# Turning the input before its root is known, and multiplying every projection by it later

## What is computed

```
h = concatenate([meta, x])                      # (272, 2048)
u = h * rsqrt(mean(h*h, axis=-1) + EPS) * attn_norm_w
z = u @ w_in[l]                                 # (272, 12368)
hq, hf, hi, hg, aq, ak, av, iq, ik, iw, ga, gb = split_cols(z, IN_SIZES)
...                                             # recurrence, indexer, attention
m = sigmoid(ga) * (y_h @ w_branch_hgrn) + sigmoid(gb) * (y_a @ w_branch_dsa)
h = h + m @ w_out
...                                             # conv-gated MLP, final norm
```

## Time and profile before

| | us |
|---|---|
| median of 3 runs (1610.62 to 1610.81) | 1610.77 |
| the profiled execution | 1610.73 |
| its span in the trace | 1609.0 |
| PE busy | 1594.9 |
| DVE busy | 961.0 |
| ACT busy | 711.3 |
| POOL busy | 94.1 |

### The profile page before, as it was taken

How to read it: one execution, slowest core, us unless ns; L and a number is a source line. 1 busy time by engine, 2 the same in 40 slices (tenths; PEclk the granted TensorE clock), 3 DMA queues, 4 the chain that set the end, 5 groups by cost and what they waited for, 6 DMA issues and landing times.

```text
span 1609.0 us, 29434 instructions
## 1 busy us (share of the span) xinstructions
PE 1594.9 (99%) x12214; PEld 1536.5 (95%) x12214; DVE 961.0 (60%) x1117; ACT 711.3 (44%) x750; POOL 94.1 (6%) x152
## 2 busy tenths in 40 slices
PE   8999999999999999999999999999999999999998
PEld 8999999999999999999999999999889999999886
DVE  7555778853355556766656666665445666666453
ACT  6333554544443335654345555454333334334332
POOL 1100050000000001111320000000000000000000
PEclk9999999999999999999999999999999999999999
DMA  7655565555464554476655555554555656465551
GB/s 236 206 158 166 163 197 177 181 174 161 153 202 158 178 165 130 144 256 218 198 179 181 186 177 188 183 182 170 196 194 174 208 161 204 159 206 190 202 208 54
DMA packets 244966, 290.36 MB, mean 180 GB/s; under 512 B 5665, under 2 KB 231186, under 8 KB 244498
## 3 DMA queue, kind: packets, MB, share of 16 engines
q1 hardware_dynamic: 238114, 278.78, 52.9%
q0 software_dynamic: 2176, 6.34, 1.2%
q10 hardware_dynamic: 4608, 4.23, 0.8%
HBM read 283.02 MB, written 6.32 MB: 180 GB/s over the span
## 4 chain that ended last, share of the span: by engine, by line
PE 98%; DVE 1%; ACT 0%; DMA 0%; issue 0%; SPq 0%; DVEq 0%; ACTq 0%
PE ps L618 24%; PE ps L619 24%; PE ps L620 24%; PE ps L1002 5%; PE ps L999 5%; PE ps L1001 5%; PE ps L948 2%; PE ps L946 2%; PE ps L947 2%; PE ps L740 1%; PE ps L715 0%; PE ps L841 0%; PE ps L938 0%; DMA x_tok<-in_x_dram 0%; PE ps L770 0%; PE ps L750 0%
## 5 line engine op out<-in xcount | busy, mean ns | idle before, releaser
L618 PE MATMUL ps<-u_hi,w_hi 128*128 128x258 f32 (+2 forms) x2944 | 841.5, 286 | 0.0
L619 PE MATMUL ps<-u_lo,w_hi 128*128 128x258 f32 (+2 forms) x2944 | 834.2, 283 | 0.0
L620 PE MATMUL ps<-u_hi,w_lo 128*128 128x258 f32 (+2 forms) x2944 | 833.8, 283 | 0.0
L1348 DVE TENSOR_TENSOR w_lo<-raw,w_hi 128x2048 fp32r<-128x2048 f32 x259 | 595.6, 2300 | 363.6 <-ACT w_hi L1043 363.3
L1043 ACT ACTIVATE w_hi<-raw 128x2048 fp32r<-128x2048 f32 x259 | 496.2, 1916 | 573.7 <-PE ps L620 408.4
L618 PEld LDWEIGHTS ps<-u_hi,w_hi 128*128 128x128 f32 x2944 | 556.0, 189 | 4.7 <-DVE z_qf L1448 2.5
L619 PEld LDWEIGHTS ps<-u_lo,w_hi 128*128 128x128 f32 x2944 | 555.9, 189 | 0.3
L620 PEld LDWEIGHTS ps<-u_hi,w_lo 128*128 128x128 f32 x2944 | 555.7, 189 | 0.0
L999 PE MATMUL ps<-w_hi,hid_hi 128*128 128x512 f32 x352 | 137.8, 391 | 0.0
L1002 PE MATMUL ps<-w_lo,hid_hi 128*128 128x512 f32 x352 | 137.1, 390 | 0.0
L1001 PE MATMUL ps<-w_hi,hid_lo 128*128 128x512 f32 x352 | 137.0, 389 | 0.0
(11 more groups left out here) (290 smaller groups left out, 1295.8 us busy)
## 6 DMA issues: line engine op xcount, KB each, us to landing
raw<-in_w_in_dram SPq DMA_DIRECT2D x48, 2048.0 KB, 8.4
raw<-in_w_ffn_gate_dram SPq DMA_DIRECT2D x22, 2048.0 KB, 8.0
raw<-in_w_ffn_up_dram SPq DMA_DIRECT2D x22, 2048.0 KB, 8.0
raw<-in_w_ffn_down_dram SPq DMA_DIRECT2D x20, 2048.0 KB, 7.7
raw<-in_w_out_dram SPq DMA_DIRECT2D x8, 2048.0 KB, 8.8
raw<-in_w_branch_hgrn_dram SPq DMA_DIRECT2D x8, 1024.0 KB, 5.4
raw<-in_w_branch_dsa_dram SPq DMA_DIRECT2D x8, 1024.0 KB, 8.5
gate_spill<-gate_st ACTq DMA_DIRECT2D x32, 129.0 KB, 3.6
```

The lines of the kernel that those rows point to most:

```text
L618: mm(acc, w_hi[s][:, k, :], mov_hi(k), start=(k == first), stop=False)
L619: mm(acc, w_hi[s][:, k, :], mov_lo(k), start=False, stop=False)
L620: ins = mm(acc, w_lo[s][:, k, :], mov_hi(k), start=False, stop=(k == last))
L1348: v.tensor_tensor(w_lo[m % 4][:], raw[(m // 2) % 2][:, :, P * (m % 2):P * (m % 2) + P], w_hi[m % 4][:].bitcast(F32), ALU.subtract).then_in ...
```

## The change

The sum of a projection is multiplied by the root where it is taken out of PSUM, so the blocks are turned and split without it.

* **Opening.** L1366, L1380, L1371, L1374 and POOL's L486 go. Meta tokens are turned first, 16 transposes into four banks, weighted by DVE into `u_meta` (4 instructions of 64 columns) and split in one step each by ACT and DVE. A "part" n of `x_part` is what ACT rounds and DVE takes the rest of at once: parts 1 to 7 are the first tile's blocks 0 to 6 (128 wide), 8 to 14 the second tile's, 15 to 23 the blocks 7 to 15 with both tiles (256 wide). The banks are seven, and the key sum moves to the eighth. Warming matmuls shrink from 18 + 4 to 2 + 4 + 2.
* **Panels in halves.** The key panel and the first query panel are each two DMAs of 8 blocks. ACT rounds the key panel in two instructions; DVE takes the first rest, POOL the second. The low-weight products of the key's second half stand behind all of its high ones, and so do those of unit 2's first half.
* **The root.** ACT squares `x_tok1` after rounding unit 3, DVE squares `x_tok2` between the halves of unit 2; one root instruction for the three tiles; DVE builds three diagonals (`diag`), PE spreads them over the partitions in one product with ones (`spread_roots`, inside unit 3), DVE copies that to `x_rs` (128 x 272).
* **Taking out.** L1394, L1414, L1448, L1482, L1483, L1617 and L1637 become products with `x_rs` instead of copies. The gates are scaled by POOL (`scale_gates`, 16 instructions of 128 x 516) when they are back from HBM.
* **Moved.** The vectors' transposes (L682) go from the front of unit 2 into unit 3, `key_squares` from unit 3 into unit 4; DVE's `rest(4)` stands ahead of the vector work instead of behind it. SP issues panel 2 when POOL and DVE have taken the key rests. `gate_st` lies elsewhere, and ACT waits for `forget_ready` before the gate units.

The diff, cut to its core:

```diff
+        def x_bank(k):
+            return ps[(k % EARLY + 4) % 7]
+        def x_part(n):
+            if n <= EARLY:
+                return n - 1, x_bank(n - 1)[:, 0:P], slice(META, END)
+            if n <= 2 * EARLY:
+                return n - EARLY - 1, x_bank(n - EARLY - 1)[:, 2 * P:3 * P], slice(END, T)
+            return n - EARLY - 1, x_bank(n - EARLY - 1)[:, 0:2 * P], slice(META, T)
...
+            sp.wait_ge(key_lo, 1)
             load(2, 0, w_cols[:, :, C_IQ + 256:C_IQ + 512])
...
-            pool.wait_ge(x_rstd, 3)
-            pool.tensor_scalar(x_tok[2][:, D // 2:], x_tok[2][:, D // 2:], rstat[:, 2:3], None, ALU.mult)\
-                .then_inc(half_normed, 1)
+            pool.wait_ge(hi_ready, 2)
+            pool.tensor_tensor(w_lo[0][:, 8:KT, 0:KEYS], raw[0][:, 8:KT, 0:KEYS], w_hi[0][:, 8:KT, 0:KEYS].bitcast(F32),
+                               ALU.subtract).then_inc(lo_ready, 2)
...
+            def scale_gates(slot, count):
+                pool.wait_ge(gate_in[slot], count)
+                pool.tensor_tensor(gates[slot][:], gates[slot][:],
+                                   x_rs[:, T0:T].rearrange("p (a t) -> p a t", a=1).to_broadcast([P, 2, TQ]), ALU.mult)\
+                    .then_inc(gate_scaled, 1)
...
+            for k in range(8):
+                keys_high(k)
+                if k + 11 < KT:
+                    turn_rest(k + 11)
+                if k == 1:
+                    pe.wait_ge(key_lo, 1)
+                    keys_low(0)
+                if k >= 1:
+                    keys_low(k)
+            pe.wait_ge(hi_ready, 2)
+            for k in range(8, KT):
+                keys_high(k)
+            pe.wait_ge(lo_ready, 2)
+            for k in range(8, KT):
+                ins = keys_low(k)
+            ins.then_inc(projected, 2)
...
+            project(3, 3, 1, T0, ((0, 3), (3, 10), (10, KT)), (spread_roots, turn_vectors))
+            pe.wait_ge(z_free, 5)
+            project(4, 0, 0, T0, ((0, 8), (8, KT)), (key_squares,))
...
+            for n in range(EARLY + 1, KT + EARLY + 1):
+                if n == 2 * EARLY:
+                    act.wait_ge(key_in, 16)
+                    round_keys(slice(0, 8))
+                if n == 2 * EARLY + 2:
+                    act.wait_ge(landed[0], landed_by[0])
+                    round_keys(slice(8, KT))
+                if n == KT + EARLY:
+                    act.wait_ge(query_in, 16)
+                    activation(w_hi[2][:, 0:8, :], raw[1][:, 0:8, 0:P], ACT.Copy).then_inc(hi_half, 1)
+                round_x(n)
...
-                v.tensor_copy(iq[:, n - U_IQ, :], ps[n % 2][:, 0:TQ]).then_inc(z_free, 1)
+                v.tensor_tensor(iq[:, n - U_IQ, :], ps[n % 2][:, 0:TQ], x_rs[:, T0:T], ALU.mult).then_inc(z_free, 1)
```

More of the change, by code:

```diff
@@ L162, in hybrid_block @@
         iq_st = [at(f"iq_st{a}", STG + 1024 * a, [P, SEQ]) for a in range(2)]
-        gate_st = [at(f"gate_st{a}", R[7] + 6144 + 1032 * a, [P, TQ]) for a in range(2)]
+        gate_st = [at(f"gate_st{a}", R[3] + 6144 + 1032 * a, [P, TQ]) for a in range(2)]
         qkv_st = at("qkv_st", STG, [P, 3, T])
@@ L639, in warm_up @@
                 for _ in range(n):
-                    mm(ps[0][:, 0:P], ones[:], ones[:], start=True, stop=True)
+                    mm(ps[7][:, 0:P], ones[:], ones[:], start=True, stop=True)
             pe.wait_ge(consts, 4)
@@ L644, in _ @@
             pe.wait_ge(norm_in, 16)
[L645 to L683, removed]
+            nc.tensor.transpose(ps[6][:, 0:KT], vec_rows[0:KT, 0, :], ident[0:KT, 0:KT]).then_inc(norm_turned, 1)
+            warm_up(2)
+            def turn(out, t, k):
+                return nc.tensor.transpose(out, x_tok[t][:, P * k:P * k + P], ident[:])
@@ new lines, in _ @@
+            pe.wait_ge(meta_zeroed, 1)
+            pe.wait_ge(x_in[0], 16)
+            for b in range(4):
+                for k in range(4):
+                    ins = turn(ps[b][:, P * k:P * k + P], 0, 4 * b + k)
+                ins.then_inc(meta_turned, 1)
+            warm_up(4)
+            pe.wait_ge(norm_ready, 1)
+            pe.wait_ge(x_in[1], 16)
+            for k in range(EARLY):
+                if k >= 3:
+                    pe.wait_ge(meta_weighted, k - 2)
+                turn(x_bank(k)[:, 0:P], 1, k).then_inc(x_turned, 1)
@@ new lines, in _, with keys_high, keys_low @@
+            keys_acc = ps[7][0:KEYS, 0:T]
+            def keys_high(k):
+                pe.wait_ge(ul_ready, k + EARLY + 1)
+                mm(keys_acc, w_hi[0][:, k, 0:KEYS], u_hi[:, k, :], start=(k == 0), stop=False)
+                mm(keys_acc, w_hi[0][:, k, 0:KEYS], u_lo[:, k, :], start=False, stop=False)
+            def keys_low(k):
+                return mm(keys_acc, w_lo[0][:, k, 0:KEYS], u_hi[:, k, :], start=False, stop=(k == KT - 1))
+            for k in range(EARLY, EARLY + 4):
+                turn_rest(k)
@@ new lines, in _, with turn_vectors, spread_roots @@
+            ins.then_inc(projected, 2)
+            def turn_vectors():
+                pe.wait_ge(vec_in, 16 * 10)
+                for n, rows in enumerate((V_A, V_B, V_C)):
+                    ins = nc.tensor.transpose(ps[4 + n][:, 0:rows], vec_rows[0:rows, n, :], ident[0:rows, 0:rows])
+                ins.then_inc(vec_turned, 1)
+            def spread_roots():
+                pe.wait_ge(x_diag, 3)
+                mm(ps[2][:, 0:T], ones[:], diag[:, P - META:3 * P], start=True, stop=True).then_inc(x_spread, 1)
@@ new lines, in round_keys @@
+            def round_keys(half):
+                activation(w_hi[0][:, half, 0:KEYS], raw[0][:, half, 0:KEYS], ACT.Copy)\
+                    .then_inc(*((key_hi, 1) if half.start == 0 else (hi_ready, 2)))
+            for n in range(1, EARLY + 1):
+                round_x(n)
+            act.wait_ge(meta_weighted, 4)
+            activation(u_hi[:, :, 0:META], u_meta[:], ACT.Copy).then_inc(meta_rounded, 1)
+            for n in range(EARLY + 1, KT + EARLY + 1):
[8 more added lines that the diff above has]
+                    activation(w_hi[2][:, 0:8, :], raw[1][:, 0:8, 0:P], ACT.Copy).then_inc(hi_half, 1)
+                round_x(n)
```

218 lines of the change are left out of this document (126 added, 92 removed).

## The result

| | before | after |
|---|---|---|
| median of 6 runs each, us | 1610.72 (1610.23 to 1610.81) | 1619.69 (1618.33 to 1627.10) |
| ratio after / before, 95% interval | | 1.0063 [1.0049, 1.0077] |
| the profiled execution | 1610.73 | 1618.33 |
| its span | 1609.0 | 1616.1 |

A forecast was written before the change was run, and what follows sets the result against it. PE was taken to bound the kernel, with only its standing still in the opening removable. Unit 5 would start at 43.3 against 46.79, 3.5 us earlier; less 0.1 for missing slack, 1610.7 - 3.4 = 1607.3 us, range 1606.6 to 1609.6.

The follow-up runs named there:

- e4: The changed kernel with POOL's scaling of the gates cut to one column instead of 516, the wait for each refill kept; 1609.68 us.
- e7: e3 with DVE's square of `x_tok2`, between the halves of unit 2's rest, done twice; 1610.76 us.
- e5: The kernel before, with POOL's merge-stage order of wait for refill, multiply (by ones), issue next refill taken over; 1614.71 us.
- e1: The changed kernel with the first two loads of `x_st` and their memsets moved ahead of POOL's merge-stage refills; 1613.45 us.
- e3: The changed kernel with DVE scaling the gates, and POOL only refilling as in the kernel before; 1607.50 us.
- e2: The changed kernel with POOL issuing each refill first and scaling the slot refilled one unit before; 1608.55 us.
- e8: e6 with the first warming block cut from 14 to 8 matmuls; 1605.64 us.
- e6: e3 without the four warming matmuls between the meta transposes and the first tile's; 1606.80 us.

## What to carry to other kernels

An added wait costs what stands behind it on the same queue, so write down, for each engine that issues DMAs, the next loads in its order and when they are needed, also those of the next stage. A loop that issues a transfer and waits for that same transfer before it issues the next runs at landing plus work; compare that with the pace of the consumer, and if it is longer, issue first and work on the transfer of one round before. An engine at 7% busy can still set the end.

## What the runs showed of the hardware

**The clock behind a wait of PE.** Waits of 1.1 (e4), 1.9 (e7) and 3.1 us (e5) left the granted clock at 1.00. The wait of 3.1 in e1 did not, and that of 8.0 in the changed kernel did not either: there the matmuls behind it started 0.21 apart. Windows of e5 and of e1 behind their waits, and one of the changed kernel inside its wait:

```profile
758.20:762.00 3.80, 3.69 (x31) 3.70 (x32) 1.65 (x2) 0.00 (x0) 0.00 (x0) 1.00 0.31 81
```

```profile
761.40:764.80 3.40, 3.40 (x18) 3.40 (x18) 0.92 (x2) 1.99 (x2) 1.47 (x3) 0.50 0.82 257
```

```profile
757.30:760.00 2.70, 0.01 (x1) 0.02 (x1) 2.19 (x2) 1.08 (x2) 2.14 (x4) 0.50 0.29 102
```

In e1 the clock was at 0.50 for 3.4 us, from just behind the restart of PE at 761.15; in the changed kernel it fell inside the wait, and 4.1 us of it lay behind the restart. The same idle time of 3.1 gave both, so a wait of some 3 us here costs itself, or itself and nearly 2 us more. The spans agree: e5's is 3.2 above before's, e1's 5.3 above e3's, of which 0.5 is its opening, 3.1 the wait, and 1.7 half of the 3.4 us at half clock.

**The first warming block.** The same 28 warming instructions behind POOL's constants took 5.01 us before, 5.17 in e5, whose opening is the same, and 5.30, 5.34, 5.48, 5.49, 5.52, 5.83 and 5.96 in kernels whose code is the same up to there; all of the opening shifts with them. This is up to 0.95 us between executions, and part of the spread of the medians. The starts show where it comes from: they are 0.213 us apart at first and 0.112 from some moment on, and that moment is 5.3 before, 5.7 in e5, 5.9 in e2 and e3, 6.2 in e8, 6.3 in the changed kernel, e6 and e7, 7.0 in e1 and 7.2 in e4. The column of the granted clock reads 1.00 on both sides of it, so in these first microseconds the pace has to be read from the starts. What sets the moment, no run shows.

**Landings of small DMAs beside large ones.** The twelve refills of 258 KB in the changed kernel land after 3.1, 6.2 and 7.0 us (least, median, most), and POOL's waits for them alternate, about 2.4 and about 5.8, without a change in the work. The issue times of SP's weight panels go with it. In the changed kernel the seven refills issued 0.8 to 2.4 us behind a panel took 6.1 to 7.0, the one issued 4.1 behind took 4.5, and the four issued more than 8 behind took 3.1 to 3.2. In the kernel before, the six issued 0.3 to 0.9 behind a panel took 6.3 to 7.2, the six issued 4.2 or more behind 3.1 to 4.5. The meta part of `x_st` fits: issued 10.4 behind a panel it landed after 2.6 (the changed kernel), 3.6 behind one after 5.7 (e5). So the rows lie; no experiment moved a panel, so that the panels delay the small DMAs is argued and not shown. The run of 1627.1 and that of 1625.18 in e5 stay unexplained. The time around the span is 2.2 to 2.6 us in the changed kernel and 2.1 to 2.5 in e1, e2 and e4, and 1.6 to 2.2 in the others; no row shows what it is.
